# Weighing and adding half of the gathered v rows on VectorE instead of TensorE in a product-key expert stage

## The reference, cut to what matters

```python
def block_fn(hb):                              # 128 tokens
    ...
    idx = jnp.take_along_axis(cand_idx, pos, axis=-1).reshape(tb, PEER_HEADS * PEER_TOPK)
    gate = jax.nn.softmax(best, axis=-1).reshape(tb, PEER_HEADS * PEER_TOPK)
    u = jnp.take(expert_u, idx, axis=0)
    act = jax.nn.gelu(jnp.einsum("tkd,td->tk", u, hb).astype(jnp.float32), approximate=False)
    vv = jnp.take(expert_v, idx, axis=0)
    return jnp.einsum("tk,tkd->td", (gate * act).astype(hb.dtype), vv)
```

## Time and profile before

| what | value |
|---|---|
| median of 3 runs | 2769.13 us (2766.65 to 2770.93) |
| span of the profiled execution | 2758.5 us |
| median less span | 10.6 us |
| TensorE busy | 2530.1 us, 92% of the span |
| VectorE busy | 1644.6 us, 60% |
| ScalarE busy | 1018.0 us, 37% |
| GpSimd busy | 842.6 us, 31% |
| moved by the gathers (queue 0) | 268.47 MB |
| chain that ended last, share of the sum's products (L2586) | 14% |

### The profile page before, as it was taken

One profiled execution on the slowest core, in us unless ns is written; L12 is line 12 of the kernel. 1 busy time (PEld: TensorE's weight loads), 2 busy tenths in 40 slices (PEclk: granted clock), 3 DMA queues, 4 the chain that ended last, 5 costly groups with the idle time before them and its releaser, 6 DMA issues.

```text
span 2758.5 us, 38393 instructions
## 1 busy us (share of the span) xinstructions
PE 2530.1 (92%) x15804; PEld 2118.2 (77%) x15804; DVE 1644.6 (60%) x3125; ACT 1018.0 (37%) x1645; POOL 842.6 (31%) x695
## 2 busy tenths in 40 slices
PE   7999999999999999999999999999978777777777
PEld 7999998999999999989999998887853233232232
DVE  6557893566566558975565552435265756566552
ACT  5444553544454445553544422622121111121121
POOL 1006870000000018740010000000056666666663
PEclk9999999999999999999999999999989787878788
DMA  6554663034545557851045554432489999999996
GB/s 218 184 174 127 182 182 100 1 127 154 189 162 183 184 138 161 178 150 62 24 148 186 189 154 134 137 118 77 150 326 378 370 372 360 378 371 365 371 370 247
DMA packets 324737, 557.41 MB, mean 202 GB/s; under 512 B 16201, under 2 KB 245587, under 8 KB 324563
## 3 DMA queue, kind: packets, MB, share of 16 engines
q1 hardware_dynamic: 250834, 286.48, 34.4%
q0 software_dynamic: 73728, 268.47, 25.4%
HBM read 553.85 MB, written 1.05 MB: 201 GB/s over the span
## 4 chain that ended last, share of the span: by engine, by line
PE 79%; DVE 8%; issue 7%; POOL 2%; ACT 1%; DMA 1%; another core or an unknown queue 1%; SPq 0%; POOLq 0%; ACTq 0%
PE bank L2586 14%; PE bank L346 12%; PE bank L437 9%; PE bank L439 9%; PE bank L438 9%; PE banks_to L437 4%; PE banks_to L439 3%; PE banks_to L438 3%; DVE banks_to L1084 3%; PE banks_to L1277 2%; DVE gdn_conv L1169 2%; PE bank L1277 2%; POOL proj L2526 1%; PE bank L759 1%; PE banks_to L2072 1%
## 5 line engine op out<-in xcount | busy, mean ns | idle before, releaser
L437 PE MATMUL bank<-operand_hi,weights_high 128*128 128x256 f32 x2528 | 715.5, 283 | 3.6 <-DVE operand_lo L876 2.0
L439 PE MATMUL bank<-operand_hi,weights_low 128*128 128x256 f32 x2560 | 716.9, 280 | 0.0
L438 PE MATMUL bank<-operand_lo,weights_high 128*128 128x256 f32 x2528 | 710.1, 281 | 0.0
L439 PEld LDWEIGHTS bank<-operand_hi,weights_low 128*128 128x128 f32 x2560 | 488.4, 191 | 0.0
L437 PEld LDWEIGHTS bank<-operand_hi,weights_high 128*128 128x128 f32 x2528 | 475.7, 188 | 7.2 <-DVE gdn_conv L1169 3.2
L438 PEld LDWEIGHTS bank<-operand_lo,weights_high 128*128 128x128 f32 x2528 | 475.8, 188 | 0.2
L393 POOL TENSOR_TENSOR weights_low<-weights,weights_high 128x1024 fp32r<-128x1024 f32 x128 | 308.0, 2440 | 445.2 <-ACT weights_high L356 445.2
L356 ACT CAST weights_high<-weights 128x1024 fp32r<-128x1024 f32 x392 | 385.9, 1044 | 0.0
L429 DVE TENSOR_TENSOR weights_low<-weights,weights_high 128x1024 fp32r<-128x1024 f32 x264 | 314.8, 1247 | 85.4 <-ACT weights_high L356 85.4
L2586 PE MATMUL bank<-weights,residual 128*128 128x512 f32 x480 | 248.5, 658 | 86.0 <-issue 84.8
L2586 PE MATMUL bank<-proj,residual 128*128 128x512 f32 x484 | 247.0, 653 | 64.9 <-issue 64.5
(11 more groups left out here) (460 smaller groups left out, 3979.5 us busy)
## 6 DMA issues: line engine op xcount, KB each, us to landing
weights<-in_ffn_w_in SPq DMA_DIRECT2D x88, 1024.0 KB, 5.0
weights<-in_mix_w_in SPq DMA_DIRECT2D x64, 1024.0 KB, 11.0
weights<-in_ffn_w_out SPq DMA_DIRECT2D x44, 1024.0 KB, 4.8
weights<-in_w_in SPq DMA_DIRECT2D x24, 1024.0 KB, 5.3
weights<-in_cnv_w_o SPq DMA_DIRECT2D x8, 1024.0 KB, 8.0
weights<-in_gdn_w_o SPq DMA_DIRECT2D x8, 1024.0 KB, 5.0
weights<-in_mix_w_out SPq DMA_DIRECT2D x8, 1024.0 KB, 5.1
weights<-in_peer_w_q SPq DMA_DIRECT2D x8, 1024.0 KB, 5.4
```

The costliest lines, as they stand in the source:

```text
L437: t.matmul(out, w_hi, x_hi, start=start, stop=False, skip_group_check=skip)
L438: t.matmul(out, w_hi, x_lo, start=False, stop=False, skip_group_check=skip)
L439: return t.matmul(out, w_lo, x_hi, start=False, stop=stop, skip_group_check=skip)
```

## The change

VectorE takes over the odd rows of each group. It multiplies a v row with its weight and adds it to a sum in SBUF (`K.scratch`, in the tile spare), one scalar_tensor_tensor of 128x1024 per row (the very first row of a token half: a tensor_scalar), behind the next group's eight dot products. TensorE sums the even rows as before, and ScalarE makes only their diagonals. At the end of each token half VectorE adds its own sum to x, then TensorE's. The weights of group i are computed in turn i of the loop, behind its dot products and the first add, instead of in turn i + 1. The steps of the choice are spread anew: one behind each dot product, two behind each add. GpSimd waits for the add of an odd row, where it waited for TensorE, before that row's home is filled again. In `scalar_scores` the gelu of group 1 stands before peer_q's last block instead of after it.

```diff
+PE_ROWS, DVE_ROWS = (0, 2, 4, 6), (1, 3, 5, 7)
...
@@ scalar_scores
-    scalar_gelu(X, m, S, K, 1)
+        if h == 6:
+            scalar_gelu(X, m, S, K, 1)
...
+def v_row_done(S, i, s):
+    return S.summed_v.at(i, s) if s in PE_ROWS else S.added_v.at(i, s)
...
@@ pool_rows
-            X.pool.wait_ge(*freed.at(*row_of(r - len(homes))))
+            X.pool.wait_ge(*done(S, *row_of(r - len(homes))))
...
@@ vector_weigh
     if i >= 2:
-        X.dve.wait_ge(*S.diag.at(i - 2, GROUP - 1))
+        X.dve.wait_ge(*S.diag.at(i - 2, PE_ROWS[-1]))
+        X.dve.wait_ge(*S.added_v.at(i - 2, DVE_ROWS[-1]))
...
+def vector_add_row(X, m, S, K, i, s):
+
+    v, w, r, sum_ = X.vector, X.dve, i * GROUP + s, K.scratch[:, i // HALF, :]
+    row, weight = K.v[r % len(K.v)][0], K.weights[i % 2][:, s:s + 1]
+    w.wait_ge(*S.weighed.at(i))
+    w.wait_ge(*S.v_in[r % len(K.v)].at(r))
+    if i % HALF == 0 and s == DVE_ROWS[0]:
+        S.added_v.by(v.tensor_scalar(sum_, row, weight, None, ALU.mult), i, s)
+        return
+    w.wait_ge(*(S.added_v.at(i - 1, DVE_ROWS[-1]) if s == DVE_ROWS[0] else S.added_v.at(i, DVE_ROWS[DVE_ROWS.index(s) - 1])))
+    S.added_v.by(v.scalar_tensor_tensor(out=sum_, in0=row, scalar=weight, in1=sum_, op0=ALU.mult, op1=ALU.add), i, s)
...
@@ vector_add_experts
-    X.dve.wait_ge(*S.summed_v.at(HALF * (t + 1) - 1, GROUP - 1))
-    x = K.x_tok[:, t, :]
+    X.dve.wait_ge(*S.added_v.at(HALF * (t + 1) - 1, DVE_ROWS[-1]))
+    S.added_v.by(X.vector.tensor_tensor(x, x, sum_, ALU.add), "x", t)
+    X.dve.wait_ge(*S.added_v.at("x", t))
+    X.dve.wait_ge(*S.summed_v.at(HALF * (t + 1) - 1, PE_ROWS[-1]))
...
@@ scalar_diagonals, tensor_group
-    for s in range(GROUP):
+    for s in PE_ROWS:
...
@@ vector_experts
             vector_dot(X, m, S, K, i, s)
-            if s == 1 and i:
-                vector_weigh(X, m, S, K, i - 1)
...
-            for _ in islice(choice, 2 if i else 3):
+            for _ in islice(choice, 1 if i else 3):
+                pass
+        for s in DVE_ROWS:
+            if i:
+                vector_add_row(X, m, S, K, i - 1, s)
+            if s == DVE_ROWS[0]:
+                vector_weigh(X, m, S, K, i)
+            for _ in islice(choice, 2):
                 pass
...
-    vector_weigh(X, m, S, K, GROUPS - 1)
+    for s in DVE_ROWS:
+        vector_add_row(X, m, S, K, GROUPS - 1, s)
     vector_add_experts(X, m, S, K, 1)
```

More of the change, by code:

```diff
@@ L111, in __init__ @@
             s(n) for n in ("u_dotted", "expert_gelu", "expert_weighed", "diagonals", "expert_sum", "expert_sum_added"))
+        self.added_v = s("v_row_weighed_and_added")
         self.last_act, self.last_dve = s("last_norm_act"), s("last_norm_dve")
@@ L2511, in row_of, with u_row_done, pool_rows @@
     return divmod(r, GROUP)
-def pool_rows(X, m, S, K, i, homes, landed, freed, table):
+def u_row_done(S, i, s):
+    return S.dotted.at(i, s)
+def v_row_done(S, i, s):
+    return S.summed_v.at(i, s) if s in PE_ROWS else S.added_v.at(i, s)
+def pool_rows(X, m, S, K, i, homes, landed, done, table):
     n, p = divmod(i, 2)
@@ L2543, in vector_weigh @@
     if i >= 2:
-        X.dve.wait_ge(*S.diag.at(i - 2, GROUP - 1))
+        X.dve.wait_ge(*S.diag.at(i - 2, PE_ROWS[-1]))
+        X.dve.wait_ge(*S.added_v.at(i - 2, DVE_ROWS[-1]))
     S.weighed.by(X.vector.tensor_tensor(K.weights[p], K.acts[p], K.gate[n % 3][:, p * GROUP:(p + 1) * GROUP], ALU.mult), i)
+def vector_add_row(X, m, S, K, i, s):
[8 more added lines that the diff above has]
+    S.added_v.by(v.scalar_tensor_tensor(out=sum_, in0=row, scalar=weight, in1=sum_, op0=ALU.mult, op1=ALU.add), i, s)
 def vector_add_experts(X, m, S, K, t):
+    x, sum_ = K.x_tok[:, t, :], K.scratch[:, t, :]
     X.dve.wait_ge(*S.score_act.at("x", 3))
-    X.dve.wait_ge(*S.summed_v.at(HALF * (t + 1) - 1, GROUP - 1))
-    x = K.x_tok[:, t, :]
+    X.dve.wait_ge(*S.added_v.at(HALF * (t + 1) - 1, DVE_ROWS[-1]))
+    S.added_v.by(X.vector.tensor_tensor(x, x, sum_, ALU.add), "x", t)
+    X.dve.wait_ge(*S.added_v.at("x", t))
+    X.dve.wait_ge(*S.summed_v.at(HALF * (t + 1) - 1, PE_ROWS[-1]))
     for half in range(2):
@@ L2569, in scalar_diagonals @@
     if i >= 2:
-        X.act.wait_ge(*S.summed_v.at(i - 2, GROUP - 1))
-    for s in range(GROUP):
+        X.act.wait_ge(*S.summed_v.at(i - 2, PE_ROWS[-1]))
+    for s in PE_ROWS:
         S.diag.by(X.scalar.activation(K.diag[p][:, s, :], m.ident[:, :], ACT.Copy, scale=K.weights[p][:, s:s + 1]), i, s)
@@ L2586, in tensor_group @@
             ins = t.matmul(m.bank[2 * half + c][:, :], K.diag[p][:, s, :], K.v[r % len(K.v)][0][:, c * 512:c * 512 + 512],
-                           start=(i % HALF == 0 and s == 0), stop=(i % HALF == HALF - 1 and s == GROUP - 1))
+                           start=(i % HALF == 0 and s == PE_ROWS[0]), stop=(i % HALF == HALF - 1 and s == PE_ROWS[-1]))
         S.summed_v.by(ins, i, s)
@@ L2598, in pool_experts @@
         if i < GROUPS:
-            pool_rows(X, m, S, K, i, K.u, S.u_in, S.dotted, io["peer_u_2"][0])
+            pool_rows(X, m, S, K, i, K.u, S.u_in, u_row_done, io["peer_u_2"][0])
         if i:
-            pool_rows(X, m, S, K, i - 1, K.v, S.v_in, S.summed_v, io["peer_v_2"][0])
+            pool_rows(X, m, S, K, i - 1, K.v, S.v_in, v_row_done, io["peer_v_2"][0])
 HALF_DONE = HALF + 2
```

## The result

The kernel after takes 2819.62 us (median of 4 runs, 2815.71 to 2825.28), the kernel before 2767.89 beside it: ratio 1.0195, 95% interval 1.0181 to 1.0209. That is slower by 2%, against a forecast of 2752.6, and outside its range of 2721 to 2802.

A forecast was written before the change was run, and what follows sets the result against it. GpSimd's gathers and pauses were taken to pace the expert stage's middle, TensorE its last 15 us. Tail -12.5, hold-ups +64, pauses -68 made -16.5 on the span 2758.5; with 10.6 outside, 2752.6 us, range 2721 to 2802.

The forecast's parts named there:

- The tail: End of the expert stage: TensorE's backlog goes and the adds from PSUM start earlier, -12.5 us (-8 to -13.5).
- The adds as work: VectorE, expert stage: 128 adds bring 5.1 us per group, fitting only if its waits shrink; counted as nothing.
- rival 2: VectorE becomes the bound in the middle, 24.4 us per group against 22.7: slower, 2802 us; chance 0.13.
- The adds beside GpSimd: GpSimd, expert stage: adds with both tensors in SBUF hold up gathers, 0.5 us each, +64 us (40 to 80 likely).
- The slow stretches: Expert stage's middle: stretches slowing every engine, ending after GpSimd pauses; nine tenths of 76 us of pauses go, -68 us.
- two feeders: Expert stage: slow stretches seem fed by transfers without a gap and by TensorE's instructions; the change weakens both.
- The sum: Whole kernel: -12.5 + 64 - 68 = -16.5 us against the span 2758.5, so 2752.6 us with the 10.6.
- The 10.6 us: Whole kernel: difference between the span 2758.5 and the runs' median 2769.1, taken as fixed.
- Moves: VectorE and ScalarE: moved weights' step hidden by an add except in slow stretches; earlier gelu gives nothing to the end.

The follow-up runs named there:

- b_tail: Kernel before, with VectorE weighing and adding odd rows only in groups 28 to 31, its sum in PSUM; 2752.3 us, ratio 0.9942.
- a_noadd: Kernel after without 126 of its 128 VectorE adds, the odd rows still gathered and waited for; 2765.95 us, ratio 0.999.
- spread kernel: Kernel after with one add behind every second dot product, for rows two groups earlier, weights and choice steps moved; first measured 2771.86 us, ratio 1.0017.
- fifth set: Runs beside a kernel before of 2689.19 us: kernel after unchanged, 2698.39 us, ratio 1.0036; with the weights' step moved back, 2700.63 us, 1.0046.
- b_flight4: Kernel before, with GpSimd waiting before each gather until no more than four are in flight; 2856.33 us, ratio 1.0328.
- b_tail24: Kernel before, with VectorE weighing and adding odd rows only from group 24 on, its sum in PSUM; 2682.33 us, ratio 0.9966.
- spread_again: The spread kernel measured once more, unchanged, beside the kernels before and after; 2778.47 us, ratio 1.0024.
- a_psum: Kernel after with h_tok in PSUM as the adds' second operand instead of the sum in SBUF, sum not formed; 2816.32 us, ratio 1.0164.
- b_flight5_again: Kernel before with at most five gathers in flight, second measurement; 2722.82 us, ratio 1.0118.

## Why the prediction was wrong

The idea of what paces the stage was right (GpSimd, its pauses, hold-ups beside adds), and so was the end. What failed is the term that was taken as nothing, VectorE's adds as work, and with it the -68 us for the pauses: GpSimd's idle time did not fall, it grew by 46.5 us.

- **The tail**, -12.5 (between -8 and -13.5): measured -11.0. Right, and b_tail shows that it is a gain of its own: -13.3 us.
- **The adds as work, "in the sum I take nothing"**: this step failed. The busy time was right (18.5 per group forecast, 18.4 measured) and so was the room for it (VectorE's waits for u rows fell from 93 to 5 us, so rival 2's sign is there: GpSimd waits for its dot products). I had written that it fits only if the 5.9 us per group of waits in slow stretches shrink, and let them shrink; they are 6.9. With that it is rival 2, to which I gave 0.13: 24.4 us per group forecast, 25.3 measured. I counted it as an average over a group. The average isn't what decides: between two groups VectorE's order has a run of adds, weights and choice steps without a dot product, and when that run falls into a slow stretch, each of its waits costs 1.4 to 4 us in the stretch shown, and up to 6.7 elsewhere. The u homes covered 10 us of the 20 there. The run comes from the moved steps and the adds together: without adds it is as long and GpSimd idles 108 us (a_noadd), with them 141.5. The spread kernel gives VectorE the same work and loses a ninth as much (1.0024 against 1.0214); in the fifth set, without slow stretches, none of GpSimd's waits for dot products is over 0.3 us.
- **The adds beside GpSimd**, +64 (40 to 80 likely, 13 the lower end): 87 gathers lengthened by 24.9 us in the kernel after, 22.9 more than before, 0.2 per add. Mis-sized: 72 gathers are caught by an add, and they meet it near its end, 0.28 us each; in the fifth set, where GpSimd doesn't stand still, 101 are caught at 0.39 each. Spread adds give the size that I had reckoned by chance, 86 to 89 us, 0.68 per add (109 caught at 0.75). A gather caught early waits for most of the add (0.94 us more at 2459.28); with the operand in PSUM none of 52 waits. The adds show no wait for a gather: those that read proj, 60 in the kernel after, take 1.284 us in the mean, as long as the one in the earlier trace rows, and none of the 126 takes over 1.35.
- **The slow stretches**, -68 of the pauses: the pauses named "remote" are gone as forecast (56 to 7 us), but the idle time isn't; it changed its name and grew by 46.5. Of the two feeders that I named, TensorE's instructions show no part (171 us of waits before steps of the choice in a_noadd, with half of the records gone, against 128 in before; TensorE idle for 20 us in the stretch shown). For the transfers without a gap no run shows one: at a DMA share of 0.91 there are no slow stretches (b_flight4), and at 1.03 there are none either (b_tail24).
- **The sum**: 24.9 - 2.0 of lengthening + 46.5 of idle time - 11.0 = +58.4, against spans of 2758.5 and 2817.2 (+58.7). The medians differ by 51.7 only. The 10.6 us that I took as fixed between span and median was not: the kernel after has 2.4, and in each of its own runs time and span differ by 1.6 to 1.7, so the profiled execution of the kernel before took about 2760 us by my estimate (2758.5 + 1.7), less than any of the four timed (2764.94 and more).
- **Moves**: the weights' step waited 1.4 us in the stretch shown, one wait among five, and 32 of the 150 us in all dot-free stretches. The steps of the choice, which the prediction had only as spread anew, waited 112. TensorE's granted clock fell from 0.80 to 0.66, and GpSimd waited 0.3 us in all for its sums: it cost nothing in the middle, as said.

## What to carry to other kernels

When work is given to an engine that has room on average, look at the longest run of its instructions that frees nothing for the engine that sets the pace, and set the buffers against that run at its slowest (here 19 to 23 us, of which the u homes covered 10 in the stretch shown), not against the mean. Give the work to it only where it pays: here in the last four groups of 32 (0.994), not in all (1.02). And when the profile shows an engine paused for "remote", count what is in flight when the pause begins and when it ends, and count the records too, before calling it a limit: in before 19 of 31 pauses begin with five gathers in flight, 13 of these end with one or two, and 1569 of 8192 records are there.

## What the runs showed of the hardware that I had not expected

- The same kernel takes 2767 to 2771 us in some sets and 2689 to 2690 in others. In the first there are at most five or six gathers of 0.52 MB in flight (5 in before, 6 in a_noadd), and of the 8192 records of their landing between 1477 (b_tail) and 7715 (b_flight4) are in the trace; in the second there are up to 14 (b_tail24), and none is missing. A change to this stage must be judged in both: the change is 1.020 and 1.021 in the one, 1.0036 in the other. What makes the kind stays open, and so does why VectorE waits up to 7.8 us for its own steps in the one (6.7 in the kernel after).
- A gather is held by a scalar_tensor_tensor of 128x1024 on VectorE with both tensors in SBUF until that operation ends (in the kernel after up to 1.99 us instead of 0.94), if it reaches a point 0.13 us after its start in that time, over 0.24 us behind the operation's start (72 of 72 in after, 109 of 109 in spread_again); not by one with an operand in PSUM (none of 52 in a_psum). The VectorE operation itself shows no wait (1.284 us in the mean, none of 126 over 1.35).
- Gathers limited to four in flight by hand give 321 GB/s in the middle (b_flight4, first kind), five 383 (b_flight5_again, second kind), no limit 409 (b_tail24, second kind).
